# Two queues instead of one for the expert weights of the first mixture

## The reference, cut to what matters

```python
def grouped_moe(h, router_w, router_bias, w_gate, w_up, w_down):
    ...
    g = jnp.argmax(group_score, axis=-1)              # each token picks one of 4 groups
    ...
    _, local = lax.top_k(in_group, TOP_K)             # and in it two of 4 experts
    ...
    for e in range(N_EXPERTS):                        # 16
        a = jax.nn.silu(hf @ w_gate[e]) * (hf @ w_up[e])
        y = y + combine[:, e:e + 1] * (a @ w_down[e])
```

## Time and profile before

| | |
|---|---|
| median of three runs | 1953.1 us |
| the profiled execution | 1955.62 us |
| its span, first to last instruction | 1953.8 us |
| TensorE busy | 1679.0 us (86%) |
| VectorE, ScalarE, GpSimd busy | 1087.9, 636.3, 272.4 us |
| mean granted clock of TensorE | 0.951 |
| DMA in all | 610.55 MB, 312 GB/s over the span |

### The profile page before, as it was taken

The page is one execution under the profiler, slowest core; times in us unless marked ns, Lnnn a source line. Parts: engine busy times, 40 slices in busy tenths (PEclk is TensorE's granted clock), DMA queues, the critical chain, the costliest instruction groups (busy, mean ns, idle before and its releaser), DMA issues.

```text
span 1953.8 us, 24600 instructions
## 1 busy us (share of the span) xinstructions
PE 1679.0 (86%) x9499; PEld 835.6 (43%) x9499; DVE 1087.9 (56%) x2222; ACT 636.3 (33%) x1105; POOL 272.4 (14%) x315
## 2 busy tenths in 40 slices
PE   4998899899989899999998997888787877688776
PEld 1876632222366574332335454783333333233332
DVE  4337722232474763224139985587666666776654
ACT  1336333433234633544431024342222222122221
POOL 0000100000000000000200000034333433343330
PEclk9999899999999989999998999899998999898998
DMA  9881399999956418999971334469999999999994
GB/s 355 291 299 44 134 396 409 409 409 410 361 180 240 169 44 349 399 398 396 400 298 57 122 116 151 140 231 424 425 423 423 424 423 423 424 423 423 424 423 209
DMA packets 154452, 610.55 MB, mean 312 GB/s; under 512 B 14280, under 2 KB 16496, under 8 KB 120800
## 3 DMA queue, kind: packets, MB, share of 16 engines
q1 hardware_dynamic: 114336, 325.98, 43.8%
q0 software_dynamic: 39296, 280.11, 34.6%
q10 hardware_dynamic: 704, 2.90, 0.4%
HBM read 607.89 MB, written 1.05 MB: 312 GB/s over the span
## 4 chain that ended last, share of the span: by engine, by line
PE 53%; DMA 28%; DVE 13%; issue 2%; ACT 2%; SPq 0%; DVEq 0%; POOLq 0%; ACTq 0%
DMA peer_rows<-in_peer_rows,MOD 18%; PE PS L997 15%; PE PS L982 8%; PE PS L1253 7%; PE PS L751 6%; PE PS L742 5%; DMA AR<-in_peer_rows,MOD 5%; DMA peer_rows<-in_down_units 2%; PE PS L772 2%; DMA peer_rows<-in_exp_w_up 2%; DVE AR L1596 2%; DMA ring<-in_w_mod 2%; PE PS L795 1%; PE PS L1044 1%; PE PS L940 1%
## 5 line engine op out<-in xcount | busy, mean ns | idle before, releaser
L1253 PE MATMUL PS<-peer_rows,HT 128*128 128x512 f32 x820 | 401.3, 644 | 113.0 <-ACT HT L1582 113.0
L2407 DVE SCALAR_TENSOR_TENSOR peer_rows<-peer_rows,PS 128x1024 f32<-128x1024 f32 x205 | 250.1, 1220 | 161.0 <-DMA peer_rows<-in_peer_rows,MOD 160.9
L1253 PEld LDWEIGHTS PS<-peer_rows,HT 128*128 128x128 f32 x820 | 164.6, 206 | 346.9 <-issue 199.2
L997 PE MATMUL PS<-peer_rows,AR 128*32 128x512 f32 (+1 forms) x1920 | 289.1, 592 | 0.1
L701 POOL DMA_INDIRECT peer_rows<-in_peer_rows,MOD x205 | 194.6, 949 | 349.7 <-PE PS L1253 296.0
L2008 DVE COPY MOD<-peer_rows 128x1024 f32 x96 | 66.5, 694 | 295.0 <-PE PS L997 103.9
L997 PE MATMUL PS<-MOD,AR 128*32 128x512 f32 x640 | 225.9, 592 | 0.0
L982 PE MATMUL PS<-peer_rows,AR 128*32 128x512 f32 x1280 | 154.1, 599 | 9.9 <-DMA peer_rows<-in_exp_w_up 5.2
L997 PEld LDWEIGHTS PS<-peer_rows,AR 128*32 128x32 f32 x1920 | 78.8, 110 | 193.0 <-issue 182.8
L1771 DVE TENSOR_TENSOR weights_low<-ring,weights_high 128x1024 fp32r<-128x1024 f32 (+1 forms) x81 | 95.6, 1196 | 108.5 <-ACT weights_high L1277 108.1
L1376 ACT ACTIVATE MOD<-peer_rows 128x1024 f32 x96 | 96.1, 1049 | 144.0 <-DMA peer_rows<-in_down_units 50.8
(11 more groups left out here) (393 smaller groups left out, 2538.1 us busy)
## 6 DMA issues: line engine op xcount, KB each, us to landing
peer_rows<-in_exp_w_gate SPq DMA_DIRECT2D x128, 512.0 KB, 8.7
peer_rows<-in_exp_w_up SPq DMA_DIRECT2D x128, 512.0 KB, 7.6
peer_rows<-in_down_units SPq DMA_DIRECT2D x128, 512.0 KB, 9.0
ring<-in_w_mod SPq DMA_DIRECT2D x20, 2048.0 KB, 9.1
ring<-in_w_in SPq DMA_DIRECT2D x7, 2048.0 KB, 8.8
ring<-in_a_w_in SPq DMA_DIRECT2D x6, 2048.0 KB, 11.3
peer_rows<-in_kv_w_mod SPq DMA_DIRECT2D x16, 512.0 KB, 10.2
peer_rows<-in_w_mod SPq DMA_DIRECT2D x16, 512.0 KB, 9.8
```

What stands on the lines that cost most here:

```text
L997: last = [nc.tensor.matmul(PS[QUARTER * i:QUARTER * i + QUARTER, banks + tile, :], left[:, tile, at + k, QUARTER * i:QUARTER * i + QUARTER ...
L1253: last = nc.tensor.matmul(PS[:, 4 + 2 * c + half, :], diagonal(k), v_row(k)[:, 512 * half:512 * half + 512], start=j == 0, stop=j == SEL - 1)
L2407: V.scalar_tensor_tensor(u_row(k), u_row(k), 1.0, PS[:, 2 * c:2 * c + 2, :].rearrange("p a k -> p (a k)"), ALU.mult, ALU.mult, accum_out=D ...
```

## The change

In the first mixture SyncE issues the units of the two larger groups (`r` = 0, 1) of every expert quad, and all of the modulation quads. GpSimd issues the units of the two smaller groups (`r` = 2, 3) from its own stream: those of the first four quads before it waits for `slots`, the others behind the accumulator fills and ahead of the two gain broadcasts. GpSimd waits for the slots by the same semaphores. Its DMAs count on semaphores of their own (`unit_pool0` to `unit_pool3`), and TensorE and VectorE wait for both; ScalarE, whose copies can only be of ranks 0 and 1, waits for SyncE's alone. The counts that `landed` gives are now added up per slot. The second mixture is as before.

```diff
+    loaded, so_far = {}, {}
+    for layer in ring_quads:
+        for m, u in enumerate(ring_quads[layer]):
+            halves = (("unit", 2), ("unit_pool", 2)) if layer == 0 and u[0] == "E" else (("unit", 4),)
+            for name, n in halves:
+                so_far[name, m % RQUADS] = so_far.get((name, m % RQUADS), 0) + 16 * n
+                loaded[name, layer, *u] = so_far[name, m % RQUADS]
+
+    def landed_pool(layer, n):
+        return f"unit_pool{ring_slot(layer, 'E', n)}", loaded["unit_pool", layer, "E", n]
+
     def landed(layer, *u):
-        return f"unit{ring_slot(layer, *u)}", 64 * ((len(ring_quads[0]) * layer + ring_no[layer, *u]) // RQUADS + 1)
+        return f"unit{ring_slot(layer, *u)}", loaded["unit", layer, *u]
...
+    def unit_source(layer, n, r, group):
+
+        kind, s, q = QUADS[n]
+        w = A[{"G": "exp_w_gate", "U": "exp_w_up", "D": "down_units"}[kind]][layer]
+        e = bass.ds(group[r] * EPG + s, 1)
...
                 for r in range(4):
...
+                    elif layer == 1 or r < 2:
+                        sp.dma_start(unit_place(slot, r), unit_source(layer, n, r, group)).then_inc(S(f"unit{slot}"), 16)
...
         load_gain("ffn0")
+        pool.wait_ge(S("order"), 1)
+        group = {r: pool.value_load(ORDER_I[0:1, r:r + 1], min_val=0, max_val=NG - 1) for r in (2, 3)}
+
+        def load_units(steps):
+            for m in steps:
+                if m >= RQUADS:
+                    sem, count = quad_free(0, m - RQUADS)
+                    pool.wait_ge(S(sem), count)
+                what, n = ring_quads[0][m]
+                if what == "E":
+                    for r in (2, 3):
+                        pool.dma_start(unit_place(m % RQUADS, r), unit_source(0, n, r, group)
+                                       ).then_inc(S(f"unit_pool{m % RQUADS}"), 16)
+
+        load_units(range(RQUADS))
         pool.wait_ge(S("slots"), 1)
         for g in range(MOD_GROUPS):
...
+        load_units(range(RQUADS, len(ring_quads[0])))
         pool.wait_ge(S("moe_used"), used(0, "U", EPG - 1, EB - 1))
         bcast(GAIN_KV, A["kv_norm_g"], "small_in")
...
                 pe.wait_ge(S(sem), count)
+                if layer == 0:
+                    sem, count = landed_pool(layer, n)
+                    pe.wait_ge(S(sem), count)
...
                 wait(*landed(layer, "E", n))
+                if layer == 0:
+                    wait(*landed_pool(layer, n))
```

More of the change, by code:

```diff
@@ L572, in build, with unit_place @@
     x_no = {"a_o": 1, "moe0": 2, "b_o": 3, "moe1": 5, "c_o": 8}
+    def unit_source(layer, n, r, group):
+        kind, s, q = QUADS[n]
+        w = A[{"G": "exp_w_gate", "U": "exp_w_up", "D": "down_units"}[kind]][layer]
+        e = bass.ds(group[r] * EPG + s, 1)
+        if kind == "D":
+            return w[e].rearrange("a h p k n -> p (a h) k n")[:, q // 2, 2 * (q % 2):2 * (q % 2) + 2, :]
+        return w[e].rearrange("a (p b) n -> p (a b) n", b=DB)[:, 2 * q:2 * q + 2, :]
+    def unit_place(slot, r):
+        return raw(slot, r).rearrange("p (b n) -> p b n", b=2)
     block = ctx.enter_context(nc.Block())
@@ L584, in load_experts @@
         def load_experts(layer, pieces_before):
-            gate, up, down = (A[n][layer] for n in ("exp_w_gate", "exp_w_up", "down_units"))
             sp.wait_ge(S("gemm_done"), pieces_before)
@@ L595, in load_experts @@
                 for r in range(4):
-                    dst = raw(slot, r)
                     if what == "M":
@@ L599, in load_experts @@
                         w, at = (A["kv_w_mod"], D * g) if g < 2 else (A["w_mod"][1], D * (g - 2))
[L600 to L609, removed]
+                        sp.dma_start(raw(slot, r), w[P * k:P * k + P, at:at + D]).then_inc(S(f"unit{slot}"), 16)
+                    elif layer == 1 or r < 2:
+                        sp.dma_start(unit_place(slot, r), unit_source(layer, n, r, group)).then_inc(S(f"unit{slot}"), 16)
         for r, s in enumerate(slabs):
```

## The result

| | median of the runs | runs |
|---|---|---|
| before | 1954.52 us | 19 |
| after | 1958.67 us (1955.13 to 1966.48) | 19 |

The ratio after to before is 1.0024, with a 95% interval of 1.0015 to 1.0033: the change costs 4.7 us (2.9 to 6.4). The time lies in the wide range given (1938 to 1963) and within the 0.5% called no change, but that range held the rivals too. The forecast's own 1941 to 1957 does not hold it, and its sign was wrong: 3.4 us gained were forecast, and a small loss is resolved. The profiled execution of the changed kernel has a span of 1956.9 us, where that of before has 1953.8.

A forecast was written before the change was run, and what follows sets the result against it. The first mixture was taken as bound by transferred bytes; terms 0 - 4.5 + 3.2 - 2.6 + 0.5 = -3.4 us gave 1949.7 us against the 1953.1 median. Own range 1941 to 1957; 8-in-10 range 1938 to 1963.

The forecast's parts named there:

- The bound: First mixture: transfers at 409 GB/s bind it; TensorE's last wait, on a late expert quad, sets its end.
- Part 1: First mixture: moving 96 of SyncE's 192 expert issues to GpSimd stays hidden behind transfers: 0 us.
- Part 2: First mixture: two queues move 417 GB/s instead of 409, 2.0% more: 4.5 us gained.
- Part 3: Late first mixture: GpSimd's queue, without modulation units, runs ahead and delays SyncE's half of the last awaited quad: +3.2 us.
- Part 4: End of first mixture: two gain broadcasts now follow GpSimd's units and land after the last awaited quad: -2.6 us.
- Part 5: First mixture: 48 waits each on TensorE and VectorE for a second semaphore, and a possible late copy: +0.5 us.
- A: First mixture: two queues fill the DMA engines to 437 GB/s; -13.4 us, 1940 us; chance 0.18.
- B: First mixture: no rate gain from two queues; +1.1 us, 1954 us; chance 0.17.
- C: First mixture: slots run dry, DMA engines idle once per period at seven modulation quads; +14.5 us, 1968 us; chance 0.13.
- D: First mixture: GpSimd's queue does not run ahead, both halves land together; sum -6.6 us, 1946.5 us; chance 0.10.
- E: First mixture: VectorE's copies delay GpSimd's issues at seven refills beside modulation quads; 4.9 us, 1954.6 us; chance 0.05.

The follow-up runs named there:

- E42: Not a run: expert quad 42, numbered from 0, of the first mixture; the forecast took TensorE's wait for its landing to set the mixture's end.
- e5: Kernel before, with every unit of the first mixture, expert and modulation, issued by GpSimd; ratio 0.9987 (0.9969 to 1.0005) to before.
- e2: Changed kernel, with modulation quads also shared, two units to each queue; ratio 1.0000 (0.9988 to 1.0013) to before.
- e15: Changed kernel run once more, unaltered, for a second profile; ratio 1.0052 (1.0036 to 1.0069) to before.
- e6: Changed kernel, with the two gain broadcasts issued earlier, where they stood in time before the change; ratio 1.0024 to before.
- E0: Not a run: the first expert quad of the first mixture, where the numbering of its 48 expert quads begins.
- e1: Changed kernel, with the two gain broadcasts held back until the last modulation quad has landed; ratio 1.0031 to before.
- e13: Changed kernel, with 20 small products keeping TensorE busy ahead of each of three expert quads it waits for; ratio 1.0030 to before.
- e8: Changed kernel, with modulation quads split three units on SyncE, one on GpSimd, expert quads still two and two; ratio 1.0026 to before.
- e3: Kernel before, with only the gain broadcasts moved behind the last modulation quad's landing; ratio 0.9995 (0.9982 to 1.0008) to before.
- e4: Changed kernel, with modulation quads shared two and two and the gain broadcasts later; ratio 0.9994 to before.
- e10: Changed kernel, with all quads, expert and modulation, split three units on SyncE and one on GpSimd; ratio 0.9983 to before.
- e17: Changed kernel, with expert quads split three units on SyncE, one on GpSimd, and modulation quads two and two; ratio 0.9991 to before.
- e7: Changed kernel, with all modulation quads issued by GpSimd instead of SyncE; ratio 1.0021 to before.
- e9: Changed kernel, with modulation quads shared two and two, gain broadcasts later and one late modulation quad issued later; ratio 0.9994 to before.
- e11: Kernel before, one queue, with gain broadcasts later and one late modulation quad issued later; ratio 0.9993 to before.
- e12: Changed kernel, with modulation quads shared two and two, gain broadcasts later and small products keeping TensorE busy in three waits; ratio 0.9998 to before.
- e16: Changed kernel, with expert quads split three units on SyncE, one on GpSimd, modulation quads whole on SyncE; ratio 1.0014 to before.
- e14: Changed kernel, with VectorE's modulation sums cut to 64 of 1024 columns, freeing slots sooner; ratio 1.0030 to before.

## Why the prediction was wrong

**The bound** was read rightly. The stage's transfers set its end, E42 is TensorE's last wait on an expert quad (M7's landing now reaches it too, by way of VectorE), and what follows the mixture moves with it nearly unchanged (1410.5 and 1411.4 us). The reading of 16.5 us from E42's slot to its landing was short: by the earlier trace rows it is 492.06 - 474.84 = 17.2, so that 9.4 us of work were queued ahead and not 8.7. No term of the sum hangs on it.

**Part 1 (issue time 0)** held. GpSimd issued 0.65 us earlier than SyncE and paid 1.11 us for two units at the end of the stage; e5, with all 224 units of 512 KB on it, cost nothing.

**Part 2 (rate with two queues, -4.5 us)** failed. Between 300 and 450 the rate was 406, with 409 before. The four us of 422 that I averaged in the earlier trace rows had gain rows of another source in GpSimd's queue, and the 433 had packets of 8 KB; the 408 was two us long. Stretches of two to four us were too short and too unlike to stand for 265. This is the step that gave the forecast its sign: without the 4.5 us the sum is +1.1. The sentence of the Trainium skill that I set aside there (DMA: Bandwidth & Descriptors, "Issuing engines are not separate DMA queues"), by which this term is 0, agrees with the 406 and with e2's 1.0000.

**Part 3 (order of landing, +3.2 us)** had the right cause, the quads that only one queue carries; its size and its place were off. e2 undoes this part alone, and the 0.24% or 4.7 us are gone. Where it failed is the sentence that at the earlier modulation quads "the engines stay full, so it is not added up". They are not full: 401 GB/s against 407 over 240 to 500, 3.8 us. The halves were 12.5 and 8.0 us in landing already at 444. In the profile of after E42's slot comes free 5.7 us late, before E42 is even issued; in e15 it is 2.5 us late, and the other 3.3 us come between slot and landing, where the forecast had put them all. The amount lies inside the bounds of 2.56 and 5.1 that were given for another reason; that is luck.

The transfers up to E42's landing show the two shares of it. These are the DMA totals and GpSimd's queue from 1 us ahead of the picks to that landing: before, after, and e6, whose broadcasts are ahead of E42.

```profile
DMA packets 29453, 107.05 MB, mean 405 GB/s; under 512 B 3382, under 2 KB 3382, under 8 KB 29430
DMA packets 29359, 106.71 MB, mean 401 GB/s; under 512 B 3370, under 2 KB 3370, under 8 KB 29336
q0 software_dynamic: 12678, 45.70, 43.4%
q0 software_dynamic: 12681, 45.72, 43.6%
```

Before, 107.05 MB took 264.0 us; after, 106.71 MB took 266.0. At the rate of before the bytes of after would have landed 0.8 us sooner; the lower rate costs 2.8 us. Of the bytes, 1.05 MB of broadcasts went and 0.7 MB came in ahead, most of it later units (GpSimd's halves of E0 to E42 are 45.1 MB): an estimated 1.8 us of the overtaking that part 3 describes. In e15 it is 107.92 MB in 269.8 us, so that the overtaking has 1.9 MB or 4.7 us, and the rate costs 3.6. E42 lands 265.0 us behind the picks in after, 268.8 in e15, 264.8 in e6, 267.1 in e1, 269.7 in e13 and 267.8 in e8; in before, e2, e3, e4, e5, e10 and e17 it is 259.5 to 263.0. So the kernels that lose are the late ones (in e7, e9, e11 and e12 the chain does not pass through this landing). e16, with its small loss, has 263.5. e14's profile does not fit (262.6); it is the fast execution named above.

**Part 4 (broadcasts behind E42, -2.6 us)** was not seen. They were issued at 513.12 and 513.76 as said, but E42 did not come earlier in the changed kernel, and the place of the broadcasts changed no ratio (e1 1.0031, e6 1.0024, after 1.0024). The two are issued just when M7 is (512.85), whose sums now stand in the chain ahead of TensorE's last wait; I had asked only when the gains are read, not what else is in the queue then. Nor may the -2.6 and the +3.2 be simply added: up to E42's landing GpSimd's queue moved 45.70 MB in after and 45.72 in e6, where the broadcasts are among them, and E42 landed at 265.0 and 264.8 us behind the picks. SyncE's half is the late one, and GpSimd's queue seems to take the same share of the engines whatever it carries; with one profile each, and 265.0 to 268.8 for one and the same kernel, this is a reading and not shown. Where SyncE's half is not alone late the term may exist: in e2, e3 and e4 E42 lands 260.8, 261.5 and 259.5 us behind the picks, before 263.0, but no ratio resolves it, and e3 leaves at most 3.5 us for it in the kernel before. That M7's later landing is due to the broadcasts, and not to the late slot, was not separated.

**Part 5 (added waits, +0.5)**: nothing shows it. E42's copy starts at 492.70, 0.07 us after the landing.

So parts 1, 2, 4 and 5, -6.6 us together by forecast, are 0.0 by e2 (-2.3 to +2.5 us), and part 3, with the lower rate that it brings, is +4.7 instead of +3.2. Both errors go the same way, and the second is the smaller.

**The rivals.** A is excluded by the rate of 406. B is right about the rate; its time of 1954 is 3.6 us under the sum that came (it took part 4 for granted). C's mechanism is shown in e15 and in part in after (a DMA share of 0.91 and 321 GB/s at 508 to 512), but not once per period, and the sum came to a third of C's: +4.7 where it had +14.5. D is excluded: GpSimd's half lands earlier at 444, and its queue has moved more than its halves of E0 to E42 (45.1 MB) when E42 lands.

E's mechanism is real and too small to count. GpSimd's issue of a unit takes 0.53 us. In after 3 of the 96 took 0.65 to 0.76, in e15 6 took 0.66 to 0.89, in e5 12 of 224 took 0.65 to 1.00; each of these 21 ran into one of VectorE's copies of 128x1024 and ended 0.12 us behind the copy's end. One of them in after, with the copy beside it:

```profile
244.29 0.75 POOL L671 DMA_DIRECT2D peer_rows<-in_exp_w_up  x1 [8.50 <-PE PS L1029]
244.23 0.69 DVE L2042 COPY MOD<-peer_rows 128x1024 f32 x1 [3.59 <-PE PS L1029]
```

In all it is 0.6 us of issue time in after and 3.1 in e5, which lost nothing. The Trainium skill (SBUF — State Buffer, the box on the "DVE blocks DMA" trap) says that GpSimd cannot write the descriptors of its DMAs during such a copy. The trace agrees in kind: the issue waits for the copy's end.

**What stays open.** Not all of the lost rate is at times when the queues are empty. Over 468 to 472 after had 346 GB/s where before had 409, and the units issued there landed after 8.9 and 9.5 us, so work was queued; at 512 to 516 it had 322 at a DMA share of 1.01, before 395 at the same share. (The dip at 264 to 272, next to M0, is in both kernels; before has it 2 us later.) Whether single engines run out of one queue's packets there was not tried. Why e8 loses as much as the whole change and e17 nothing is open as well. No version is shown to be faster than before by an amount worth having: e10 is the best, 0.9983, with an interval that ends at 0.9997, and as one of seventeen it may be chance.

## What to carry to other kernels

Two queues onto the same DMA engines bring no rate when one keeps them at 409 GB/s. If a ring of slots is filled from two queues, divide every slot, fillers included, in the same proportion: that cost nothing here, while four of the five unequal divisions tried cost 0.14% or more. A queue that runs ahead moves pieces that are not yet wanted, and the late piece sets the time. Take a rate for a sum from the longest stretch of the same packets, and for a transfer moved later ask what else is in flight at the new place, and whether its queue is the late one.

## What the runs showed of the hardware

- GpSimd's queue moves these units as fast as SyncE's: all of them on it (e5) gave 406 GB/s over 240 to 500, where before had 407.
- GpSimd's issue of a unit takes 0.53 us, and 0.65 to 1.00 when it runs into one of VectorE's copies of 128x1024; it then ends 0.12 us behind the copy (21 issues in after, e15 and e5).
- The shares of the two queues follow what is queued. At 444 to 448 it is 52.9% to 49.8% in after, and with one unit in four on GpSimd (e10) 78.8% for SyncE's queue and 23.1% for GpSimd's, as in these rows:

```profile
q1 hardware_dynamic: 349, 1.25, 78.8%
q0 software_dynamic: 91, 0.37, 23.1%
```

- After a wait of 9.4 us (e15) TensorE's granted clock was 0.50 at 500 to 506, the lower of its two levels (1.2 GHz of 2.4), and 1.00 again from 509. The quad behind the wait took 8.08 us where it takes 5.15.
- One kernel's profiles differ: the stage of the changed kernel varied between 317.8 and 320.7 us in two profiles, and its ratio in two sets of runs was 1.0024 (1.0015 to 1.0033) and 1.0052 (1.0036 to 1.0069). The interval of one set does not hold all of the spread.
